# Copying v rows beside turned u rows, so that an expert slot is fetched in one piece of 8 KB instead of two of 4 KB

## The chip, the cores and the metric

The kernel runs on one core of one Trainium2 chip. The metric is device time in microseconds (us): the median of several runs, with one more execution recorded by the hardware profiler. Engines are named as in the profile: PE (TensorE), DVE (VectorE), ACT (ScalarE), POOL (GpSimd), SP (SyncE, which only issues transfers). The profile also counts the core's 16 DMA engines, which move all data between HBM and the on-chip memory.

## The reference

One step of a small backbone with two layers, for 128 context tokens and 256 latent tokens, 384 tokens of 1024 numbers in all, in float32. Each layer runs a mixer (attention, a chunked recurrent scan, a short convolution) and then PEER, a table of 16384 tiny experts per layer. It is PEER's tables that the change touches:

```python
def peer_ffn(h, wq, subkeys, u_tab, v_tab):        # per chunk of 128 tokens
    q = (xt @ wq).reshape(PEER_CHUNK, PEER_HEADS, 2, PEER_HALF)
    sc = jnp.einsum('thpd,hpnd->thpn', q, subkeys)
    ...                                            # top 16 of 256 pairs, per head: expert numbers e, weights g
    act = jax.nn.gelu(jnp.einsum('thkd,td->thk', u_tab[e], xt))
    return jnp.einsum('thk,thkd->td', g * act, v_tab[e])
```

A token has 8 heads with 16 experts each, 128 slots; for every slot a row of u and a row of v (1024 numbers, 4 KB each) are needed. Over 384 tokens and two layers that is 805 MB of gathered rows.

## The kernel before, in words

Tokens lie in 3 tiles of 128, one token per partition. The program runs in stages, each closed by a barrier of all engines: `begin` (once: the input norm and the conditioning products with w_ada, 24 pieces of 1 MB), then for each of the two layers `project` (the input projection, 20 output blocks), `attention`, `rwkv`, `output`, `scoring` (queries, keys, the top 16 of each half), `experts` and `finish`.

**The row turning.** v arrives from the host with one expert per row. u arrives transposed, so each layer turns its u table while the earlier stages run. The table is cut into 128 units, called rows in the code, of 128 experts, 512 KB each. For one unit ACT's queue issues a load into one of 4 buffers (`rows_load`, L261), PE transposes it in 8 pieces of 128x128 into two banks of its own (`rows_pe`, L288), ACT copies the two banks out (`rows_act`, L303) into one of 3 buffers, and ACT's queue issues the store into an HBM tensor `u_rows` (`rows_store`, L274). The load for unit m + 4 is issued behind the copies of unit m; the store of unit m ahead of the copies of unit m + 1; the copies of unit m wait for the store of unit m - 3.

**Where units are turned.** PE and ACT both run their programs in order, and the calls `rows_pe(c, pe, count)` and `rows_act(c, act, count)` stand at fixed places in them. The counts are the constants `IN_BEGIN`, `IN_PROJECT` and so on (L36). Per layer they give: 18 units in `begin` (only in layer 0), 20 in `project` (one behind each output block on PE; on ACT two behind every second block, after that block's weight split L508), 18 in `attention`, 48 in `rwkv`, 8 in `output`, 16 in `scoring`. In layer 0 that is 128. In layer 1 it is 110, and `rows_pe(c, pe, NK)` at the end of `scoring` turns the last 18 there (L1617, L1563). `rows_end` waits until all stores have landed, since `experts` reads the table.

**The experts.** A layer has 384 slots (3 tiles x 128). For each, POOL issues two indirect transfers, one row per token: the u half from `u_rows` and the v half from the input v (L1693), into one of 9 buffers of 128 x 8 KB. For slot n it first waits until PE is done with slot n - 9 (`slot_done`). DVE multiplies the u half with the tokens and sums (L1726), ACT applies the gelu and makes a diagonal matrix of the weights (L1835, L1826), PE multiplies it with the v half and accumulates (L1857). DVE waits for the semaphore `landed` of the u half, PE for `landed_v` of the v half. DVE and ACT take slots in groups of 2, and the weights of a group are made after the next group's sums. Between groups of the first tiles DVE also picks the experts of the next tile (`select`). In layer 0 the weights w_ada of layer 1 come in here too.

Of the kernel before, what the change touches and what calls it, by code (L numbers as in the profile page):

```python
# [10 lines left out]
P = 128  # L11
# [21 lines left out]
SLOTS_OF_TOKEN = PH * TOPK  # L33
GROUP = 2
BUFS = 9
IN_BEGIN, IN_PROJECT, IN_SCORES, IN_VALUES, IN_GRAMS, IN_LEVEL, IN_CHUNKS, IN_SCAN, IN_OUT, IN_Q = 1, 1, 2, 1, 1, 2, 2, 1, 1, 1  # L36

SLOTS = 4
PIECE = 2048
# [66 lines left out]
def make_core(nc, ctx, dram):  # L106
    c = Core()
    c.nc, c.dram = nc, dram
    sb = lambda name, shape, dt=F32: ctx.enter_context(nc.sbuf_tensor(name, shape, dt))
    sem = lambda name: ctx.enter_context(nc.semaphore(name))  # L110
    c.ring = sb("ring", [P, SLOTS, PIECE])
    c.ident = sb("ident", [P, P])
    c.hT = sb("hT", [P, KD, TOK])
    c.mod_cols = sb("mod_cols", [P, 4, KD, 2])
    c.ring_full = [sem(f"ring_full{i}") for i in range(SLOTS)]
    c.att_tables_in, c.rwkv_tables_in = sem("att_tables_in"), sem("rwkv_tables_in")
    c.late_in, c.ident_in = sem("late_in"), sem("ident_in")
    c.rows_came = [sem(f"rows_came{i}") for i in range(ROWS_IN)]
    c.rows_kept = [sem(f"rows_kept{i}") for i in range(ROWS_OUT)]
    c.rows_full, c.rows_free = [[sem(f"rows_{n}{i}") for i in range(2)] for n in ("full", "free")]  # L120
    c.landed = [sem(f"landed{i}") for i in range(BUFS)]
    c.landed_v = [sem(f"landed_v{i}") for i in range(BUFS)]
    c.x_dram = nc.dram_tensor("x_between_blocks", [TILES, P, D], F32, kind="Internal").ap()
    c.gate_dram = nc.dram_tensor("gate_rows", [DEPTH + 1, 2, 2, D], F32, kind="Internal").ap()
    c.u_rows = nc.dram_tensor("u_rows", [DEPTH * NK // 2, P, 2 * D], F32, kind="Internal").ap()
    c.silu, c.ones = sb("cond_silu", [P, KD, 2]), sb("ones", [1, 2])
    return c

# [133 lines left out]
        c.rows_came[m % ROWS_IN], 16)  # L262


def rows_begin(c, act):

    for m in range(c.rows.first, c.rows.first + ROWS_IN):
        rows_load(c, act, m)


def rows_store(c, act, m):

    act.wait_ge(c.rows_free[1], m + 1)
    act.dma_start(c.u_rows[m // 2, :, (m % 2) * D:(m % 2 + 1) * D], c.rows.turned[:, m % ROWS_OUT, :]).then_inc(  # L274
        c.rows_kept[m % ROWS_OUT], 16)


# [15 lines left out]
def rows_act(c, act, count):  # L293

    r = c.rows
    for m in range(r.by_act, min(r.by_act + count, r.end)):
        if m > r.first:
            rows_store(c, act, m - 1)
        if m >= ROWS_OUT:
            act.wait_ge(c.rows_kept[m % ROWS_OUT], 16 * (m // ROWS_OUT))  # L300
        for q in range(2):
            act.wait_ge(c.rows_full[q], m + 1)
            c.nc.scalar.copy(r.turned[:, m % ROWS_OUT, 512 * q:512 * q + 512], r.bank[q][:, :]).then_inc(c.rows_free[q], 1)  # L303
        if m + ROWS_IN < r.end:
            rows_load(c, act, m + ROWS_IN)
    r.by_act = min(r.by_act + count, r.end)


def rows_end(c, act):

    rows_store(c, act, c.rows.end - 1)
    for i in range(ROWS_OUT):
        act.wait_ge(c.rows_kept[i], 16 * len(range(i, c.rows.end, ROWS_OUT)))


def begin(c):

    nc, dram = c.nc, c.dram
    with ExitStack() as ctx:
# [11 lines left out]
        with nc.Block() as block:  # L331
# [15 lines left out]
            def _(act):  # L347
# [11 lines left out]
                    ada_pair_copy(c, s, act, rows, t)  # L359
                for m in range(TILES, N_ADA // PAIR):  # L360
                    ada_pair_copy(c, s, act, rows, m)
                    rows_act(c, act, PAIR * IN_BEGIN)
                for t in range(TILES):
                    act.wait_ge(S["normed"], t + 1)
                    act.dma_start(c.x_dram[t], x[:, t, :]).then_inc(S["stored"], 16)
# [29 lines left out]
            def _(pe):  # L395
# [2 lines left out]
                pe.wait_ge(S["bias_in"], 16)  # L398
                for m in range(N_ADA // PAIR):
                    ada_pair_product(c, s, pe, rows, piece_full, m)  # L400
                    if m >= TILES:
                        rows_pe(c, pe, PAIR * IN_BEGIN)
                ada_transposes(c, s, pe, rows, PAIR)
                pe.wait_ge(S["normed"], TILES)
                for t in range(TILES):
# [37 lines left out]
def project(c, l, pT, att, rw):  # L443
# [3 lines left out]
    with ExitStack() as ctx:  # L447
# [4 lines left out]
        with nc.Block() as block:  # L452
# [8 lines left out]
            def _(act):  # L461
# [5 lines left out]
                for m in range(N_PIN):  # L467
                    b, r = at("proj", 2 * m)
                    act.wait_ge(full[b], r + 1)
                    nc.scalar.copy(pT[:, 2 * m, :], bank[b][:, 0:TOK]).then_inc(free[b], 1)  # L470
                    if m + 2 < N_PIN:
                        split_high(c, s, act, AT_IN, m + 2, ws, at("proj", 2 * m + 1))
                    rows_act(c, act, 2 * IN_PROJECT)

            @block.vector
            def _(dve):
# [1144 lines left out]
def experts(c, l, h_tok, top, idx, acc, late):  # L1621
# [11 lines left out]
    with ExitStack() as ctx:  # L1633
# [28 lines left out]
        shifted = spare(2 * ST).bitcast(U32).rearrange("p (w k) -> p w k", w=2)  # L1662

        BEFORE = l * TILES * ST
        u_rows = c.u_rows[0:(l + 1) * NK // 2].rearrange("a p (two n) -> (a p two) n", two=2)
        v_rows = dram["v"].rearrange("l a p (two n) -> (l a p two) n", two=2)

        def buffer_of(n):
            return uv[(BEFORE + n) % BUFS]
# [12 lines left out]
        with nc.Block() as block:  # L1682

            @block.gpsimd
            def _(pool):
                for n in range(TILES * ST):
# [2 lines left out]
                        pool.wait_ge(S["routed"], 2 * t + 1)  # L1689
                    if n >= BUFS:  # L1690
                        pool.wait_ge(S["slot_done"], n - BUFS + 1)
                    for table, half, came in ((u_rows, 0, c.landed), (v_rows, 1, c.landed_v)):
                        nc.gpsimd.indirect_dma_start(buffer_of(n)[:, half * D:half * D + D], None, table,  # L1693
                                                     bass.IndirectOffsetOnAxis(eid[:, t, k:k + 1], 0)).then_inc(came[landing(n)], 16)

            @block.sync
            def _(sp):
# [150 lines left out]
            def _(pe):  # L1848
                if not last:
                    pe.wait_ge(S["bias_in"], 16)  # L1850
                for j in range(GROUPS):
                    for n in range(j * G, j * G + G):
                        t, k = divmod(n, ST)
                        pe.wait_ge(c.landed_v[landing(n)], landings(n))
                        pe.wait_ge(S["diag_done"], n + 1)
                        for h in range(2):
                            ins = nc.tensor.matmul(acc[2 * t + h][:, :], diag[:, n % DIAGS, :],  # L1857
# [215 lines left out]
```

## Time and profile before

| | us |
|---|---|
| median of 3 runs (3779.28 to 3791.21) | 3790.41 |
| the profiled execution, device time | 3795.43 |
| its span, first to last instruction | 3793.6 |
| busy: PE matmul | 2767.8 (73%) |
| busy: DVE | 1900.8 (50%) |
| busy: POOL | 1615.3 (43%) |
| busy: ACT | 945.0 (25%) |

The profiled execution took 5.0 us more than the median of the three runs. A busy share is an average over stages of very different kinds. The profile has further lines for the DMA engines: their mean busy share over the span in 40 slices, what they moved, and the share of each queue. Queue q0 holds the indirect transfers that POOL issues, q10 the plain ones of ACT, q1 those of SP. PEclk is TensorE's granted clock as a share of full speed.

### The profile page before, as it was taken

What the parts mean: (1) busy time and instruction counts of PE and PEld (TensorE: products, weight loads), DVE (VectorE), ACT (ScalarE), POOL (GpSimd) and SP (SyncE); (2) the same over time, 40 slices, a digit from 0 to 9 for tenths busy, and PEclk for the clock granted to TensorE, in tenths of its full rate; (3) what the DMA queues carried; (4) which work ended last, traced back from release to release, by engine and by line L of the source; (5) the groups of instructions that cost most, each with busy time, mean ns of one, the idle gap of its engine ahead of it and who ended that gap; (6) DMA issues with size and microseconds to landing.
All of it is one profiled execution on the core that took longest, in us unless ns stands there. A gap on an engine that the chain in (4) does not pass through costs nothing. (4 is left out here: it accounts for less than half of the span.)

```text
span 3793.6 us, 36906 instructions
## 1 busy us (share of the span) xinstructions
PE 2767.8 (73%) x12342; PEld 1703.0 (45%) x12342; DVE 1900.8 (50%) x4344; ACT 945.0 (25%) x2400; POOL 1615.3 (43%) x1578
## 2 busy tenths in 40 slices
PE   5686797774777888888758769969366777777775
PEld 3575686761222333333227658859222222222221
DVE  1114655488644444444452355556485444444445
ACT  2334443331111111111123344334211111111111
POOL 0001000006777777777720100000177777777774
PEclk7797798887899999999979779979599999999998
DMA  9756466658999999999975547656799999999996
GB/s 387 304 198 202 139 243 245 230 213 301 351 397 409 411 411 410 410 408 407 409 277 202 185 157 258 233 215 211 275 353 362 400 409 407 409 406 409 408 408 254
DMA packets 323469, 1206.61 MB, mean 318 GB/s; under 512 B 39370, under 2 KB 41930, under 8 KB 311250
## 3 DMA queue, kind: packets, MB, share of 16 engines
q0 software_dynamic: 221184, 805.40, 54.1%
q10 hardware_dynamic: 75328, 274.86, 20.5%
q1 hardware_dynamic: 26772, 123.99, 8.5%
q8 instruction: 103, 1.69, 0.2%
q14 instruction: 82, 0.67, 0.0%
HBM read 1061.47 MB, written 142.64 MB: 317 GB/s over the span
## 5 line engine op out<-in xcount | busy, mean ns | idle before, releaser
L1857 PE MATMUL acc<-exp_uv,exp_diag 128*128 128x512 f32 x3072 | 1462.8, 623 | 618.8 <-ACT exp_diag L1826 618.5
L1726 DVE CUSTOM_DVE_ANT_0 exp_uv<-exp_uv,h_tok 128x1024 f32<-128x1024 f32 x768 | 940.8, 1226 | 1001.9 <-DMA exp_uv<-u_rows,exp_eid 1000.4
L1693 POOL DMA_INDIRECT exp_uv<-u_rows,exp_eid x768 | 784.9, 1022 | 1270.2 <-DVE exp_eid L1801 1006.7
L1857 PEld LDWEIGHTS acc<-exp_uv,exp_diag 128*128 128x128 f32 x3072 | 577.3, 197 | 1492.9 <-issue 1492.9
L1693 POOL DMA_INDIRECT exp_uv<-in_v,exp_eid x768 | 791.8, 1031 | 234.4 <-issue 234.4
L1835 ACT ACTIVATE exp_gel<-exp_dot 128x2 f32<-128x2 f32 x384 | 78.6, 205 | 1732.3 <-DVE exp_dot L1726 1732.3
L303 ACT COPY rows<-rows_bank 128x512 f32<-128x512 f32 x512 | 277.8, 589 | 418.7 <-PE rows_bank L288 312.8
L288 PE MATMUL rows_bank<-ident,rows 128*128 128x128 f32 x2048 | 310.3, 301 | 98.2 <-ACT rows L303 98.2
L288 PEld LDWEIGHTS rows_bank<-ident,rows 128*128 128x128 f32 x2048 | 258.1, 156 | 143.0 <-issue 140.5
L1826 ACT ACTIVATE exp_diag<-ident,exp_w 128x128 f32<-128x128 f32 x768 | 260.9, 388 | 0.1
L552 PE MATMUL project_bank<-project_hs,project_ws 128*128 128x384 f32 x960 | 188.1, 353 | 32.4 <-DVE project_hs L540 32.4
L655 POOL TENSOR_TENSOR att_conv_z<-pT 128x768 f32<-128x768 f32 x2 | 3.6, 1799 | 472.3 <-POOLq L99 472.3
L552 PEld LDWEIGHTS project_bank<-project_hs,project_ws 128*128 128x128 f32 x960 | 176.6, 200 | 33.2 <-DVE project_hs L540 33.2
L552 PE MATMUL score_bank<-score_xs,score_ws 128*128 128x384 f32 x768 | 146.8, 347 | 6.7 <-DVE score_xs L540 6.7
L552 PEld LDWEIGHTS score_bank<-score_xs,score_ws 128*128 128x128 f32 x768 | 137.4, 195 | 7.2 <-DVE score_xs L540 7.2
L1465 PE MATMUL output_bank<-output_ws,output_hs 128*128 128x256 f32 x576 | 81.0, 303 | 39.5 <-DVE output_hs L540 39.2
L483 DVE COPY pT<-project_bank 128x384 f32<-128x384 f32 x20 | 11.2, 558 | 188.8 <-PE project_bank L552 188.8
L1465 PEld LDWEIGHTS output_bank<-output_ws,output_hs 128*128 128x128 f32 x576 | 77.4, 210 | 41.0 <-issue 40.3
L158 PE MATMUL exp_bank<-ring,cond_silu 128*2 128x256 f32 x384 | 86.8, 379 | 0.0
L1277 PE MATMUL rwkv_bank<-rwkv_Dm,rwkv_Ak 128*128 128x128 f32 x480 | 65.6, 300 | 14.1 <-DVE rwkv_Ak L1096 14.1
L1122 DVE TENSOR_TENSOR rwkv_Dm<-rwkv_Dm,rwkv_bank 128x384 f32<-128x384 f32 x64 | 35.2, 549 | 71.3 <-PE rwkv_bank L1289 71.3
L1277 PEld LDWEIGHTS rwkv_bank<-rwkv_Dm,rwkv_Ak 128*128 128x128 f32 x480 | 63.3, 215 | 15.3 <-DVE rwkv_Ak L1096 15.3
(296 smaller groups left out, 2556.0 us busy)
## 6 DMA issues: line engine op xcount, KB each, us to landing
rows<-in_u ACTq DMA_DIRECT2D x256, 512.0 KB, 5.6
u_rows<-rows ACTq DMA_DIRECT2D x256, 512.0 KB, 5.2
ring<-in_w_ada SPq DMA_DIRECT2D x48, 1024.0 KB, 8.0
ring<-in_w_in SPq DMA_DIRECT2D x20, 1024.0 KB, 8.5
ring<-in_wq SPq DMA_DIRECT2D x16, 1024.0 KB, 6.8
exp_uv<-u_rows,exp_eid POOLq DMA_INDIRECT x768, 6.6
exp_uv<-in_v,exp_eid POOLq DMA_INDIRECT x768, 6.6
ring<-in_w_out SPq DMA_DIRECT2D x8, 1024.0 KB, 12.5
```

The lines of the kernel that those rows point to most:

```text
L158: ins = c.nc.tensor.matmul(out, c.silu[:, k, :], w[:, k, :], start=False, stop=(k == KD - 1))
L288: ins = c.nc.tensor.transpose(r.bank[q][:, k * P:(k + 1) * P], r.came_in[:, m % ROWS_IN, f * P:(f + 1) * P], c.ident[:, :])
L303: c.nc.scalar.copy(r.turned[:, m % ROWS_OUT, 512 * q:512 * q + 512], r.bank[q][:, :]).then_inc(c.rows_free[q], 1)
L552: ins = c.nc.tensor.matmul(s.bank[b][:, 0:TOK], w[:, a, n % 2, k, :], hs[:, v, k, :], start=(k == 0 and i == 0), stop=(k == KD - 1 and i = ...
L1122: nc.vector.tensor_tensor(dst[:, g, hh, :, :], dst[:, g, hh, :, :], bank[b][:, 0:TOK].rearrange("p (t n) -> p t n", t=TILES), ALU.add).the ...
L1277: ins = mm(bank[b][:, tile_cols(t)], Ak[:, g, hh, t, :], Dm[:, g, hh, t, :], start=True, stop=True)
L1465: ins = nc.tensor.matmul(bank[b][:, 0:NW], hs[:, v, k, t * P:(t + 1) * P], w[:, a, k, :], start=(k == 0 and i == 0), stop=(k == KD - 1 and ...
L1693: nc.gpsimd.indirect_dma_start(buffer_of(n)[:, half * D:half * D + D], None, table, bass.IndirectOffsetOnAxis(eid[:, t, k:k + 1], 0)).then ...
L1726: V.tensor_tensor_reduce(buffer_of(n)[:, 0:D], buffer_of(n)[:, 0:D], h_tok[:, t, :], 1.0, 0.0, ALU.mult, ALU.add, dot[:, j % 8, n % G:n % ...
L1826: nc.scalar.activation(diag[:, n % DIAGS, :], c.ident[:, :], ACT.Identity, scale=w[:, j % 8, n % G:n % G + 1]).then_inc(S["diag_done"], 1)
L1835: nc.scalar.activation(gel[:, j % 8, :], dot[:, j % 8, :], ACT.Gelu_apprx_tanh).then_inc(S["gelu_done"], 1)
L1857: ins = nc.tensor.matmul(acc[2 * t + h][:, :], diag[:, n % DIAGS, :], buffer_of(n)[:, D + 512 * h:D + 512 * h + 512], start=(k == 0), stop ...
```

## The change

An HBM tensor `uv_rows` takes the place of `u_rows`. Each expert has a row of 8 KB in it, the u row and then the v row. The store of a turned unit writes the u halves. A new transfer per unit (`rows_join`), issued by ACT behind the unit's load, copies the 512 KB of the same experts' v from the input into the v halves, from HBM to HBM; all of them count on one semaphore, `joined`, for which `rows_end` waits. In `experts` POOL issues one indirect transfer per slot, of rows of 8 KB, where it issued two, and DVE and PE wait for the same semaphore.

The places of the units change too. `begin` turns none. `project` turns 40: two behind each output block on PE, and on ACT two right behind each block's copy, one call ahead of the weight split and one behind it. With 18, 48, 8 and 16 in the other stages that is 130 places, so both layers are done with their 128 units two blocks ahead of the end of `scoring`.

```diff
-IN_BEGIN, IN_PROJECT, IN_SCORES, ... = 1, 1, 2, ...
+IN_PROJECT, IN_SCORES, ... = 2, 2, ...
...
-    c.u_rows = nc.dram_tensor("u_rows", [DEPTH * NK // 2, P, 2 * D], F32, kind="Internal").ap()
+    c.uv_rows = nc.dram_tensor("uv_rows", [DEPTH * NK // 2, P, 2, 2, D], F32, kind="Internal").ap()
...
+def rows_join(c, act, m):
+
+    j = m % NK
+    act.dma_start(c.uv_rows[m // 2, :, m % 2, 1, :], c.dram["v"][m // NK, j // 2, :, (j % 2) * D:(j % 2 + 1) * D]).then_inc(c.joined, 16)
...
-    act.dma_start(c.u_rows[m // 2, :, (m % 2) * D:(m % 2 + 1) * D], c.rows.turned[:, m % ROWS_OUT, :]).then_inc(
+    act.dma_start(c.uv_rows[m // 2, :, m % 2, 0, :], c.rows.turned[:, m % ROWS_OUT, :]).then_inc(
...
         if m + ROWS_IN < r.end:
             rows_load(c, act, m + ROWS_IN)
+        rows_join(c, act, m)
...
+    act.wait_ge(c.joined, 16 * c.rows.end)
...
                 for m in range(TILES, N_ADA // PAIR):
                     ada_pair_copy(c, s, act, rows, m)
-                    rows_act(c, act, PAIR * IN_BEGIN)
...
                     ada_pair_product(c, s, pe, rows, piece_full, m)
-                    if m >= TILES:
-                        rows_pe(c, pe, PAIR * IN_BEGIN)
...
                     nc.scalar.copy(pT[:, 2 * m, :], bank[b][:, 0:TOK]).then_inc(free[b], 1)
+                    rows_act(c, act, IN_PROJECT)
                     if m + 2 < N_PIN:
                         split_high(c, s, act, AT_IN, m + 2, ws, at("proj", 2 * m + 1))
-                    rows_act(c, act, 2 * IN_PROJECT)
+                    rows_act(c, act, IN_PROJECT)
...
-                    for table, half, came in ((u_rows, 0, c.landed), (v_rows, 1, c.landed_v)):
-                        nc.gpsimd.indirect_dma_start(buffer_of(n)[:, half * D:half * D + D], None, table,
-                                                     bass.IndirectOffsetOnAxis(eid[:, t, k:k + 1], 0)).then_inc(came[landing(n)], 16)
+                    nc.gpsimd.indirect_dma_start(buffer_of(n)[:, :], None, uv_rows,
+                                                 bass.IndirectOffsetOnAxis(eid[:, t, k:k + 1], 0)).then_inc(c.landed[landing(n)], 16)
...
-                        pe.wait_ge(c.landed_v[landing(n)], landings(n))
+                        pe.wait_ge(c.landed[landing(n)], landings(n))
```

ACT's order in `project`, from the copy of the first output block on. Here `pT` takes the projection, `project_ws` the split weights, and a DMA row is a transfer that ACT's queue issues. Before:

```order
L470 COPY pT<-project_bank 128x384
L508 CAST project_ws<-ring 128x2048
L274 DMA u_rows<-rows 128x1024
L303 COPY rows<-rows_bank 128x512 x2
L261 DMA rows<-in_u 128x1024
L274 DMA u_rows<-rows 128x1024
L303 COPY rows<-rows_bank 128x512 x2
L261 DMA rows<-in_u 128x1024
L470 COPY pT<-project_bank 128x384
```

And in the changed kernel, the same stretch up to the middle of the second half piece:

```order
L475 COPY pT<-project_bank 128x384
L309 COPY rows<-rows_bank 128x512 x2
L261 DMA rows<-in_u 128x1024
L268 DMA uv_rows<-in_v 128x1024
L280 DMA uv_rows<-rows 128x1024
L309 COPY rows<-rows_bank 128x512 x2
L261 DMA rows<-in_u 128x1024
L268 DMA uv_rows<-in_v 128x1024
L514 CAST project_ws<-ring 128x2048
L280 DMA uv_rows<-rows 128x1024
L309 COPY rows<-rows_bank 128x512 x2
```

Between two copies into `pT` ACT had 2 units and 4 transfers; it has 4 units (two stand here ahead of the weight split and two follow behind it) and 12 transfers, the added kind being the copy of v (L268).

PE's order at the end of `begin` and the start of `project` (`begin_bank` takes the conditioning products, `rows_bank` the turned pieces). Before:

```order
L187 MATMUL begin_bank<-begin_rows,ones 2x128 x4
L190 MATMUL begin_bank<-ring,cond_silu 2x128 x32
L288 MATMUL rows_bank<-ident,rows 128x128 x16
L213 MATMUL begin_bank<-ident,begin_rows 128x2 x32
L568 MATMUL begin_bank<-ident,begin_x 128x128 x24
...
L552 MATMUL project_bank<-project_hs,project_ws 128x384 x24
L288 MATMUL rows_bank<-ident,rows 128x128 x8
L552 MATMUL project_bank<-project_hs,project_ws 128x384 x24
```

And in the changed kernel:

```order
L187 MATMUL begin_bank<-begin_rows,ones 2x128 x4
L190 MATMUL begin_bank<-ring,cond_silu 2x128 x32
L213 MATMUL begin_bank<-ident,begin_rows 128x2 x32
L574 MATMUL begin_bank<-ident,begin_x 128x128 x24
...
L558 MATMUL project_bank<-project_hs,project_ws 128x384 x24
L294 MATMUL rows_bank<-ident,rows 128x128 x16
L558 MATMUL project_bank<-project_hs,project_ws 128x384 x24
```

The 16 transposes (2 units) behind each of the last nine conditioning products are gone, and each projection block is followed by 16 instead of 8.

## Rows read from the trace of the kernel before

**Rows 1.** The page's slices of the span: DMA busy tenths, GB/s.

```profile
DMA  9756466658999999999975547656799999999996
GB/s 387 304 198 202 139 243 245 230 213 301 351 397 409 411 411 410 410 408 407 409 277 202 185 157 258 233 215 211 275 353 362 400 409 407 409 406 409 408 408 254
```

**Rows 2.** DMA view, 3000 to 3700 us (experts, layer 1): queue, packets, MB, share of 16 engines.

```profile
q0 software_dynamic: 78381, 285.41, 102.4%
...
exp_uv<-u_rows,exp_eid POOLq DMA_INDIRECT x273, 6.6
exp_uv<-in_v,exp_eid POOLq DMA_INDIRECT x273, 6.6
```

**Rows 3.** Costliest groups, same stretch: busy, mean ns of one, idle before and releaser.

```profile
L1857 PE MATMUL acc<-exp_uv,exp_diag 128*128 128x512 f32 x1089 | 502.9, 605 | 198.8 <-ACT exp_diag L1826 198.8
L1726 DVE CUSTOM_DVE_ANT_0 exp_uv<-exp_uv,h_tok 128x1024 f32<-128x1024 f32 x272 | 333.3, 1226 | 354.1 <-DMA exp_uv<-u_rows,exp_eid 354.1
L1693 POOL DMA_INDIRECT exp_uv<-u_rows,exp_eid x273 | 279.1, 1022 | 83.1 <-issue 83.1
L1693 POOL DMA_INDIRECT exp_uv<-in_v,exp_eid x273 | 256.7, 940 | 83.3 <-issue 83.3
```

**Rows 4.** DMA view, 60 to 120 us (begin): queue, packets, MB, share.

```profile
DMA packets 5193, 25.22 MB, mean 420 GB/s; under 512 B 579, under 2 KB 579, under 8 KB 3661
...
q10 hardware_dynamic: 3469, 12.63, 51.7%
q1 hardware_dynamic: 1718, 12.50, 49.6%
```

**Rows 5.** Stretches: length, busy of PE, PEld, DVE, ACT, POOL (instructions), PEclk, DMA share, GB/s.

```profile
2667.00:2703.00 36.00, 24.68 (x112) 20.06 (x110) 0.30 (x3) 15.05 (x29) 0.00 (x0) 0.59 0.98 398
154.00:282.00 128.00, 106.93 (x622) 103.88 (x620) 23.92 (x18) 40.56 (x57) 0.00 (x0) 0.93 0.60 206
1990.00:2114.00 124.00, 103.03 (x619) 100.15 (x617) 23.92 (x18) 40.11 (x57) 0.00 (x0) 0.96 0.59 206
2800.00:2900.00 100.00, 68.05 (x136) 26.68 (x136) 74.34 (x180) 16.32 (x54) 79.59 (x68) 0.93 0.96 352
```

**Rows 6.** Timeline, last product of begin: start, length, engine, line, idle before and releaser.

```profile
114.72 3.59 PE L190 MATMUL begin_bank<-ring,cond_silu 128*2 128x128 f32 x64
118.40 0.59 ACT L303 COPY rows<-rows_bank 128x512 f32<-128x512 f32 x1 [5.75 <-DMA u_rows<-rows]
...
122.67 2.10 PE L213 MATMUL begin_bank<-ident,begin_rows 2*128 2x2 f32 x32
```

**Rows 7.** Timeline, end of scoring in layer 1.

```profile
2667.02 0.28 DVE L1587 FIND_INDEX8 idx<-top,score_sc 128x8 uint32<-128x128 f32 x1
...
2702.48 0.33 ACTq L274 DMA_DIRECT2D u_rows<-rows  x1
2706.72 0.33 SPq L1698 DMA_DIRECT2D exp_iota<-in_iota  x1
```

**Rows 8.** Timeline, a pair of units in project.

```profile
176.44 1.07 ACT L303 COPY rows<-rows_bank 128x512 f32<-128x512 f32 x2
...
177.16 1.94 PE L288 MATMUL rows_bank<-ident,rows 128*128 128x128 f32 x8 [2.62 <-ACT rows L303]
177.53 0.33 ACTq L274 DMA_DIRECT2D u_rows<-rows  x1
```

**Rows 9.** Line L303 alone (two copies per unit) by stretch: ACT busy (count), PEclk, DMA share, GB/s.

```profile
350.00:377.00 27.00, 8.66 (x16) 0.98 0.84 267
484.00:536.00 52.00, 17.20 (x32) 1.00 0.86 300
590.00:624.00 34.00, 10.75 (x20) 1.00 0.80 281
657.00:714.00 57.00, 8.61 (x16) 0.89 0.69 278
722.00:834.00 112.00, 17.22 (x32) 0.93 0.63 221
```

More of the change, by code:

```diff
@@ L35 @@
 BUFS = 9
-IN_BEGIN, IN_PROJECT, IN_SCORES, IN_VALUES, IN_GRAMS, IN_LEVEL, IN_CHUNKS, IN_SCAN, IN_OUT, IN_Q = 1, 1, 2, 1, 1, 2, 2, 1, 1, 1
+IN_PROJECT, IN_SCORES, IN_VALUES, IN_GRAMS, IN_LEVEL, IN_CHUNKS, IN_SCAN, IN_OUT, IN_Q = 2, 2, 1, 1, 2, 2, 1, 1, 1
 SLOTS = 4
@@ L121, in make_core @@
     c.landed = [sem(f"landed{i}") for i in range(BUFS)]
-    c.landed_v = [sem(f"landed_v{i}") for i in range(BUFS)]
+    c.joined = sem("joined")
     c.x_dram = nc.dram_tensor("x_between_blocks", [TILES, P, D], F32, kind="Internal").ap()
     c.gate_dram = nc.dram_tensor("gate_rows", [DEPTH + 1, 2, 2, D], F32, kind="Internal").ap()
-    c.u_rows = nc.dram_tensor("u_rows", [DEPTH * NK // 2, P, 2 * D], F32, kind="Internal").ap()
+    c.uv_rows = nc.dram_tensor("uv_rows", [DEPTH * NK // 2, P, 2, 2, D], F32, kind="Internal").ap()
     c.silu, c.ones = sb("cond_silu", [P, KD, 2]), sb("ones", [1, 2])
@@ L1664, in experts @@
         BEFORE = l * TILES * ST
-        u_rows = c.u_rows[0:(l + 1) * NK // 2].rearrange("a p (two n) -> (a p two) n", two=2)
-        v_rows = dram["v"].rearrange("l a p (two n) -> (l a p two) n", two=2)
+        uv_rows = c.uv_rows[0:(l + 1) * NK // 2].rearrange("a p two w n -> (a p two) (w n)")
         def buffer_of(n):
```

## The prediction

> **What bounds the kernel now.** I began with the slices of the span [rows 1]. They show two long plateaus, slices 12 to 20 and 32 to 39, at 397 to 411 GB/s with the DMA engines at nine tenths or more: the two `experts` stages. Between them the engines are half idle (139 to 304 GB/s), except in the first slice and at the end of the second `scoring`. So the reader should see two kinds of stage, and ask of each edit in which kind it lies.
>
> For the plateau I took a calm stretch without expert picking. In 700 us POOL issues 273 u fetches and 273 v fetches, so a slot takes 2.564 us; the indirect queue is busy for 102.4% of the stretch and moves 285.41 MB, that is 285.41 / (1.024 x 700 us) = 398 GB/s of full share [rows 2]. The groups say the rest [rows 3]: PE is busy for 503 of 700 us and DVE for 333, DVE's idle time ends on the fetch, PE's on ACT's diagonals, which follow DVE. POOL has no gap either: 279.1 + 256.7 busy and 83.1 + 83.3 of issue make 702 us. The v issues take 940 ns and the u issues 1022, so POOL alone could go at 2 x (0.940 + 0.305) = 2.49 us a slot. Transfers and their issue both stand close to the slot's 2.56 us, and a gain there needs both.
>
> For the other kind I took the price of one 512 KB transfer with the DMA engines full. In `begin`, ACT's queue moves 12.63 MB in 51.7% of 60 us, 407 GB/s of full share; SP's queue, whose pieces are 8 KB, moves 12.50 MB in 49.6%, 420 GB/s [rows 4]. At the end of `scoring` in layer 1 ACT's transfers alone make 398 GB/s at a share of 0.98, 406 again [rows 5]. So a load or a store of a unit costs 0.524 MB / 407 GB/s = 1.29 us, and a turned unit 2.58 us of the DMA engines. In `project` the share is only 0.60 and 0.59 [rows 5]: there the units are hidden today.
>
> **The change, part by part. The first stage.** 18 units leave `begin`, where the DMA engines are full: 18 x 2.58 = 46 us. PE's last product starts at 114.7 us, and the transposes behind it, at 122.7, follow a unit that waited 5.75 us for a store [rows 6]. What is late next is w_ada itself: a pair of pieces, 2.1 MB at 420 GB/s, takes 5.0 us against 3.59 us of product, so the DMA engines still set the pace and nearly all of the 46 come out. I take -45.
>
> **The end of scoring.** In layer 1 DVE is done at 2667.3 us; the last store is issued at 2702.5 and `experts` starts at 2706.7 [rows 7]. These 39 us go, less some 2 for the barrier: -37. Two units fewer inside each `scoring` save PE a little, -2 per layer.
>
> **The fetch.** The bytes stay. If an 8 KB row gains as SP's 8 KB pieces do over ACT's 4 KB pieces, 420 / 407 = 1.032, the slot falls from 2.564 to 2.485 us, -0.08 x 768 = -61 us. If it went at 420 GB/s outright it would be 1.049 MB / (420 x 1.024) = 2.44 us, -96; if the row is moved as two pieces as before, nothing. Issue no longer holds it: one issue in place of two is about 1.3 us per slot. While DVE picks experts the rate is only 352 GB/s at a share of 0.96 [rows 5], and there the gain is smaller. I take -55, with 0 and -96 as ends. DVE now waits for the v half too; behind it in its program stand the next sums and weights, and PE waits for those, but the DMA engines move the same bytes in a slot, so this costs one half fetch at the start of a layer, about 1.3 us, which I leave out.
>
> **The copy of v.** No row shows an HBM to HBM transfer. It cannot be cheaper than one pass, 1.29 us, the price of the same 128 pieces of 4 KB as a load or as a store. If its reading and its writing come one after the other in whatever is full, it costs a load and a store, 2.58 us. What is nearest? In `begin` loads and stores are mixed, at the end of `scoring` they are half and half, in `experts` there are loads alone, and all come to 398 to 420 GB/s of HBM reading plus writing [rows 2, 4, 5]. A store's write does not ride free beside a load's read. An engine that is busy per piece would look the same, so these rows do not decide it; I take 2.58, since by count of HBM bytes the copy is nearest to a unit's load and store. The Trainium skill's page DMA: Bandwidth & Descriptors, section Latency and other measured facts, has 207 to 214 GB/s per direction for copies between two HBM tensors. By it the copy would be 0.524 MB / 214 = 2.45 us, an estimate, and the sum below 20 us less; no run here shows it yet.
>
> The copies are issued on ACT's queue, ahead of later loads and stores. PE meets a unit in its program order and waits for its load; behind it stand the projection's blocks. So a full queue stops the projection itself.
>
> **Project.** The share of 0.60 over 128 us is 77 us of transfers: 20 units x 2.58 = 52, and 25 for w_in and tables [rows 5]. Afterwards it is 40 x (2.58 + 2.58) + 25 = 231 us. Some lies outside: four loads are issued ahead, and the last stores and copies land later; I count three units, 15 us. 216 in place of 128 is +88 us per layer (+40 with the cheap copy: 40 x 3.87 + 25 - 12 = 168). PE is not the bound: a unit with its wait on ACT takes it at most 1.94 us [rows 8], so 20 more are 39 us, 167 in all. ACT's issues take 0.33 us each and its copies 0.59 [rows 6, 8]; 40 units x (2 x 0.59 + 3 x 0.33) is 87 us, well inside.
>
> **The other stages.** Their units stay, but each brings a copy. The dense runs [rows 9], where two copies on ACT are one unit: 16 units from 484 to 536 us need 0.86 x 52 + 16 x 2.58 = 86 us, 34 too much, of which three units (15) can wait in buffers: +19. From 590 to 624: 27 + 10 x 2.58 = 53, +4 by the same rule. From 350 to 377: 23 + 8 x 2.58 = 43, +1. `output`: 39 + 21 = 60 in 57, +3. In `scoring` 0.63 x 112 + 14 x 2.58 - 2 x 2.58 = 102 stays under 112 and is hidden; that slack also covers the new wait for `joined`, since the last unit comes two blocks before the end. Together +27 per layer, or +2 with the cheap copy.
>
> **The sum.** 2 x (88 + 27) = +230; -45 - 37 - 4 - 55 = -141; net +89. 3795.4 + 89 = 3884 for a profiled execution; the median lay 5.0 below its profile, so 3880 us, 2.4% slower.
>
> **The rivals.** *The copy costs one pass.* Then a layer loses 40 + 2, two lose 84, and the gains of 141 win: -57, 3733 us. For it speaks that each load and store now fills the engines alike, whichever end is HBM, as if the pieces were the cost. Against it, the byte count above. The line between: the loss per layer goes from 42 to 115 while the copy goes from 1.29 to 2.58, and it equals half of 141 at about 1.8 us. Below that the change is faster.
>
> *The wide fetch gains nothing*, because each row is still moved as two pieces, or because nine buffers, of which a slot now holds one until the whole row is there, hold POOL back. POOL never waits for PE in the calm stretch [rows 3], which speaks against the second. With the dear copy: 3880 + 55 = 3935.
>
> *The turned units stay hidden.* This is the hope that the half-idle stages have room: per layer `project` to `scoring` has it on average. It needs the copies to be spread; in `project` alone they ask for more than the stage has, so I see it only as part of the cheap copy: a price of about 1.8 us, 3790 us, no change.
>
> **How the numbers follow.** Dear copy with the gain 0.51 (3880; its own range 3850 to 3920), dear copy without it 0.09 (3935), near the line 0.07 (3790), cheap copy 0.33 (3733, or 3710 to 3760 by the fetch's ends). A measurement of this kernel tells about 0.3%, 11 us, from no change. Faster 0.33, same 0.07, slower 0.60. The range 3720 to 3940 leaves out the tails of the outer cases, below 2 in 10.
>
> **What would show it.** Right: in the two `project` stages a DMA share near 1, PE waiting for units on the load of u, some 215 us in place of 128 in each; ACT's queue with a third of transfers more and at 2 to 2.6 us each; `begin` ending near 78 in place of 123 us; `experts` following `scoring` without the 39 us; a slot at 2.45 to 2.5 us. Wrong: a copy at 1.3 us with `project` near 170 us; a slot that stays at 2.56; `begin` still ending past 100 us, if PE or ACT take over there.

## The result and the profile after

The changed kernel takes 3742.54 us, the median of 4 runs (3735.49 to 3744.95), beside 3790.06 us for the kernel before on the same chip: a ratio of 0.9878 with a 95% interval of 0.9855 to 0.9901, 1.2% faster where 2.4% slower was forecast. It came out 9.5 us above the first rival, the copy that costs one pass (3733). The profiled execution took 3744.95 us, its span 3743.1; before it was 3795.4, so 50.5 us went.

The slices of the changed kernel's span, DMA busy tenths and GB/s, answer to [rows 1]:

```profile
DMA  8997599686999999999969876986689999999996
GB/s 346 368 404 265 214 364 332 266 304 260 420 420 419 417 416 420 418 417 419 420 271 404 340 272 230 345 323 264 229 329 420 420 415 420 420 417 420 416 415 249
```

The plateaus of `experts` went from some 408 to some 419 GB/s, and `project` (slices 3, 22 and most of 23, counted from one) became full. Stage by stage, from the first to the last instruction with the turned units left aside, read from the two timelines (us). `project` counts from its first to its last copy into `pT`, `output` from its first product to its last step on ACT ahead of the norm (`output_rstd`):

| stage | before, layers 0 / 1 | after | change |
|---|---|---|---|
| start to the first copy of `pT` in `project` | 155.0 | 120.3 | -34.7 |
| project | 126.6 / 123.4 | 155.3 / 154.9 | +28.7 / +31.5 |
| project's end to attention | 2.6 / 2.4 | 7.0 / 7.3 | +4.4 / +4.9 |
| attention | 90.8 / 91.6 | 101.2 / 106.5 | +10.4 / +14.9 |
| rwkv | 270.6 / 270.5 | 276.1 / 279.2 | +5.5 / +8.7 |
| output | 57.3 / 56.8 | 63.0 / 63.7 | +5.7 / +6.9 |
| scoring | 111.8 / 111.9 | 110.6 / 110.8 | -1.2 / -1.1 |
| scoring's end to experts, layer 1 | 39.4 | 1.7 | -37.7 |
| experts | 1106.1 / 1057.3 | 1057.5 / 1008.1 | -48.6 / -49.2 |

**Project.** The DMA view of the changed kernel, 130 to 250 us (layer 0): queue, packets, MB, share of 16 engines; then issues by kind with the median time to landing.

```profile
q10 hardware_dynamic: 12351, 44.96, 93.7%
q1 hardware_dynamic: 576, 4.19, 8.4%
...
uv_rows<-rows ACTq DMA_DIRECT2D x29, 512.0 KB, 10.0
rows<-in_u ACTq DMA_DIRECT2D x29, 512.0 KB, 8.9
uv_rows<-in_v ACTq DMA_DIRECT2D x29, 512.0 KB, 10.1
```

29 stores, 29 loads and 29 copies share the queue, and 44.96 MB / (0.937 x 120 us) is 400 GB/s: 0.524 MB / 400 = 1.31 us of the engines for each transfer, close to the 1.29 of [rows 4], with a third of them copies. The times to landing (8.9 to 10.1 us) are some seven times this price: about as many transfers are under way at once, an estimate. The stretches of the changed kernel (columns of [rows 5]) show the half-idle stages filled, and the waits of 120 to 276 us show what ends ACT's waiting there:

```profile
120.00:276.00 156.00, 128.41 (x770) 122.85 (x768) 23.92 (x18) 60.37 (x95) 0.00 (x0) 0.92 1.02 405
1960.00:2115.00 155.00, 124.49 (x768) 119.19 (x767) 23.64 (x18) 60.04 (x94) 0.00 (x0) 0.94 1.02 407
283.00:384.00 101.00, 68.81 (x403) 56.69 (x404) 38.80 (x94) 42.11 (x111) 15.65 (x17) 0.70 0.77 274
388.00:664.00 276.00, 219.08 (x1734) 194.71 (x1734) 157.03 (x318) 105.33 (x225) 2.87 (x2) 0.89 0.81 295
743.00:854.00 111.00, 96.94 (x616) 95.99 (x616) 80.94 (x395) 49.39 (x77) 0.00 (x0) 0.93 0.75 270
```

```profile
ACT rows L309 <- DMA uv_rows<-rows: 56.2, 29, 4.6
...
PE rows_bank L294 <- ACT rows L309: 27.4, 21, 2.7
```

ACT waits for the store of a unit three before, which lies in the queue behind copies. PE's own waits there end on ACT's copies out of its banks, and none is put down to a load. The transfers alone fill the stage: from the first to the last copy into `pT` the q10 queue moves 57.30 MB, 109 of the 120 transfers, at 1.31 us each, and w_in takes 13 us more, 156 in all.

**The fetch.** The DMA view of 2950 to 3650 us (a calm stretch, as [rows 2]), POOL's group there (as [rows 3]), and the stretch with expert picking that [rows 5] has at 352 GB/s:

```profile
q0 software_dynamic: 40106, 292.09, 101.0%
...
exp_uv<-uv_rows,exp_eid POOLq DMA_INDIRECT x279, 11.6
```

```profile
L1697 POOL DMA_INDIRECT exp_uv<-uv_rows,exp_eid x279 | 294.1, 1054 | 407.6 <-PE acc L1861 404.1 <-issue 3.5
```

```profile
2800.00:2900.00 100.00, 75.15 (x158) 29.83 (x159) 78.06 (x193) 18.74 (x63) 44.64 (x40) 0.97 1.01 420
```

A slot takes 700 / 279 = 2.509 us, 0.055 less. POOL, which had no gap, now waits 404 of 700 us for PE to free a buffer: issue has stopped being a limit. In the picking stretch it had been the limit: 68 issues of 79.59 us together and 0.3 us of issue time after each fill the 100 us of [rows 5]. Now 40 issues of 44.64 us suffice, and the stretch moves 420 GB/s in place of 352, 40 slots in place of 34. The next tiles' experts are picked while some 50 slots at the start of each layer are worked off; the first 96 slots of a layer gained 32 us, the other 288 some 18.

**The first stage.** PE's last product of `begin` and what follows it, as [rows 6], and two stretches ahead of it; then the waits of 20 to 92 us on SP:

```profile
88.37 3.27 PE L190 MATMUL begin_bank<-ring,cond_silu 128*2 128x128 f32 x64
93.03 2.42 PE L213 MATMUL begin_bank<-ident,begin_rows 2*128 2x2 f32 x32 [1.39 <-ACT begin_rows L200]
```

```profile
40.00:60.00 20.00, 9.18 (x236) 5.94 (x228) 0.00 (x0) 4.11 (x16) 0.00 (x0) 0.83 0.82 321
60.00:80.00 20.00, 10.51 (x216) 6.37 (x216) 0.00 (x0) 2.64 (x11) 0.00 (x0) 0.68 0.79 318
```

```profile
SPq L350 <- PE begin_bank L190: 54.8, 9, 9.0
```

The transposes start at 93.0 in place of 122.7 us. The engines are not full any more: SP may not issue a pair of pieces before the product of the pair that held its place in the four-slot ring, and spends 54.8 us on that.

### The profile page after: what moved, and what is told of

Its sections match the earlier page's. It is cut to its first block and busy times, and to the rows that moved or that the text cites. A ratio compares the mean times of both kernels' runs of the same rounds, so it can differ in the third digit from the quotient of the medians.

```text
span 3743.1 us, 36396 instructions
## 1 busy us (share of the span) xinstructions
PE 2738.1 (73%) x12342; PEld 1698.9 (45%) x12342; DVE 1901.3 (51%) x4344; ACT 940.4 (25%) x2400; POOL 884.8 (24%) x810
## 5 line engine op out<-in xcount | busy, mean ns | idle before, releaser
L1861 PE MATMUL acc<-exp_uv,exp_diag 128*128 128x512 f32 x3072 | 1431.9, 612 | 559.3 <-ACT exp_diag L1830 559.3
L1697 POOL DMA_INDIRECT exp_uv<-uv_rows,exp_eid x768 | 846.1, 1102 | 2115.8 <-PE acc L1861 1102.2
L1861 PEld LDWEIGHTS acc<-exp_uv,exp_diag 128*128 128x128 f32 x3072 | 566.3, 193 | 1413.4 <-issue 1413.1
L294 PE MATMUL rows_bank<-ident,rows 128*128 128x128 f32 x2048 | 295.9, 292 | 102.1 <-ACT rows L309 101.8
L294 PEld LDWEIGHTS rows_bank<-ident,rows 128*128 128x128 f32 x2048 | 246.3, 150 | 142.8 <-issue 139.9
L521 DVE TENSOR_TENSOR project_ws<-ring,project_ws 128x2048 fp32r<-128x2048 f32 x20 | 45.8, 2292 | 39.4 <-ACT project_ws L514 39.4
```

Of the source, the lines that this page charges most:

```text
L294: ins = c.nc.tensor.transpose(r.bank[q][:, k * P:(k + 1) * P], r.came_in[:, m % ROWS_IN, f * P:(f + 1) * P], c.ident[:, :])
L521: c.nc.vector.tensor_tensor(ws[:, b, 1, :], c.ring[:, slot(first + m), :], ws[:, b, 0, :].bitcast(F32), ALU.subtract).then_inc(s.named["w_ ...
L1697: nc.gpsimd.indirect_dma_start(buffer_of(n)[:, :], None, uv_rows, bass.IndirectOffsetOnAxis(eid[:, t, k:k + 1], 0)).then_inc(c.landed[land ...
```

## The experiments

**Theory**: a copy of v costs the DMA engines about what a load costs, so the loss is small and the one fetch pays for it. **Rivals**: the copy is dear, and something else gave the time; `project` is long because of 20 more units on PE and ACT, not because of the copies; the fetch is worth only its 2.2% in a calm slot.

**move** is the kernel before with the placement alone:

```diff
-IN_BEGIN, IN_PROJECT, ... = 1, 1, ...
+IN_PROJECT, ... = 2, ...
...
+                    rows_act(c, act, IN_PROJECT)
                     if m + 2 < N_PIN:
...
-                    rows_act(c, act, 2 * IN_PROJECT)
+                    rows_act(c, act, IN_PROJECT)
```

> Only the placement of the turning is changed: none in begin, two half pieces a block in project, no unit left behind scoring. u is stored in its old table, v is not copied, a slot is fetched in two 4 KB halves as before. The first stage should end about 35 us earlier and the 38 us behind the second scoring should go, -75 together with scoring itself. Theory that the copies are what lengthens project: project needs 62 - 21 = 41 MB at 400 GB/s, 103 us, is again bound by PE and ACT and takes 126 to 140 us a layer; attention, rwkv and output stay at 91, 271 and 57; total 3715 to 3745. Rival, that the twenty additional units a project lengthen it by their turns on PE and ACT whatever the copies do: project at 155 us as in the changed kernel, total about 3775.

3738.48 us, ratio 0.9861 (0.9828 to 0.9894). `project` takes 135.2 us a layer, attention 94.8, rwkv 270.6, output 57.4. Its stretch:

```profile
119.00:254.00 135.00, 116.83 (x766) 112.01 (x765) 23.88 (x18) 59.90 (x95) 0.00 (x0) 1.00 0.93 328
```

So the units alone lengthen `project` by some 10 us and the copies by 20, and the placement alone has the whole net gain. Of attention's loss 3 to 4 us a layer come with the placement too. PE's granted clock is 1.00 here and 0.92 in the changed kernel's `project`, where PE is busy for 128 us in place of 117; but there the transfers alone add up to the stage's length.

**two_fetches** is the changed kernel with u and the copied v in two tables and two 4 KB fetches a slot:

```diff
-    c.uv_rows = nc.dram_tensor("uv_rows", [DEPTH * NK // 2, P, 2, 2, D], F32, kind="Internal").ap()
+    c.u_rows = nc.dram_tensor("u_rows", [DEPTH * NK // 2, P, 2 * D], F32, kind="Internal").ap()
+    c.v_rows = nc.dram_tensor("v_rows", [DEPTH * NK // 2, P, 2 * D], F32, kind="Internal").ap()
...
-                    nc.gpsimd.indirect_dma_start(buffer_of(n)[:, :], None, uv_rows,
+                    for table, half, came in ((u_rows, 0, c.landed), (v_rows, 1, c.landed_v)):
+                        nc.gpsimd.indirect_dma_start(buffer_of(n)[:, half * D:half * D + D], None, table,
```

> The changed kernel with u and v rows in two tables and a slot fetched in two 4 KB halves; the copies of v and the placement stay. Theory that the 98 us that both experts stages lost came from the one 8 KB fetch: experts back at 1106 and 1057 us, a calm slot at 2.56 us, the stretches with expert picking back at 352 and 375 GB/s; total 3742 + 98 = 3840. Rival, that the fetch is worth the 2.2 per cent of the calm slot alone (0.055 us x 768 = 42 us) and the rest came with the placement: 3785.

3835.72 us, 1.0135 (1.0095 to 1.0174). `experts` is back at 1107.8 and 1049.4 us, and its picking stretch (the same place in layer 1) at 361 GB/s with POOL full:

```profile
2842.00:2942.00 100.00, 71.14 (x139) 27.80 (x138) 75.37 (x180) 17.08 (x57) 78.84 (x70) 0.91 0.97 361
```

The theory holds: the one fetch is worth 3835.7 - 3742.5 = 93 us. And with two fetches on both sides, the copies cost 3835.7 - 3738.5 = 97 us in all. The two halves of the table cancel.

**old_places** completes the square: copies and one fetch, with the units placed as before.

```diff
+                    rows_act(c, act, PAIR * IN_BEGIN)
...
+                    if m >= TILES:
+                        rows_pe(c, pe, PAIR * IN_BEGIN)
```

> The other half of the change alone: v copied beside u and one 8 KB fetch a slot, with the turning placed as in the kernel before (18 units in begin, one half piece fewer in project, a tail behind scoring). The placement alone gave 3738, both together 3743, the kernel before 3790. If the two halves add, this one is worth about +4: 3794. If the copies in begin and in the tail behind the second scoring, where the DMA engines are full, cost more than those that leave project: 18 x 1.3 and 10 x 1.3 us, less up to 2 x 20: 3790 to 3800. If the fetch's 98 us were had for less there: below 3770.

3786.97 us, 0.9981 (0.9959 to 1.0003): no change that can be told. `begin` ends 22 us later than before (first `pT` copy at 177.2) and the wait behind the second scoring grows from 39 to 65 us, where the copies meet full engines (a DMA share of 1.02 in `begin`, 0.98 behind `scoring`), while `project` with its 20 units stays at 125.0. So placement is worth 52 us without the table and 44 with it.

**copies_alone** issues layer 0's 128 copies in a stage of their own, ahead of `begin`.

```diff
+            for m in range(NK):
+                rows_join(c, act, m)
+            act.wait_ge(c.joined, 16 * NK)
...
-        rows_join(c, act, m)
+        if m >= NK:
+            rows_join(c, act, m)
```

> A stage ahead of the first one issues layer 0's 128 copies of v one behind the other, with nothing else on the DMA engines; layer 0's other stages then carry no copies, layer 1 is as in the changed kernel. One pass a copy: 128 x 1.31 = 168 us for the stage, near 400 GB/s; and with layer 0 losing its 50 us (project 155 to about 130, attention 101 to 91, rwkv 276 to 271, output 63 to 57), total 3742 + 168 - 50 = 3860. A load and a store a copy: 128 x 2.58 = 330 us, total about 4020. The Trainium skill, page DMA: Bandwidth & Descriptors, section Latency and other measured facts, has 207 to 214 GB/s for HBM to HBM; by it the stage would be 67.1 MB / 214 = 314 us, an estimate.

3904.97 us; the stages that follow start 215 us later, and layer 0's `project` takes 135.1 us, as in `move`. The DMA view of 20 to 200 us:

```profile
q10 hardware_dynamic: 16009, 58.30, 100.8%
```

58.30 / (1.008 x 180) = 321 GB/s, 1.63 us a copy: between the theories, and dearer than the 1.31 of `project`. The Trainium skill's page DMA: Bandwidth & Descriptors, section Latency and other measured facts, has 214 GB/s per direction as the full rate of copies between HBM tensors, measured on pieces of 16 KB at a padded row pitch of 4 MB. These copies, of 4 KB pieces that lie closer, went well above it, and for them the measurement decides.

**prices, prices_paced, prices_long** ask why. Each adds a stage with nothing else on the engines and issues transfers in a chosen order, the first with the queue full, the second with at most four under way, the third with 128 rounds in `project`'s order. The first lines are of `prices`, the others of `prices_long`.

```diff
+            for m in range(3 * each, 4 * each):
+                load(m, range(4))
+                store(m, range(4, 7))
+                rows_join(c, act, m)
...
+            for m in range(NK):
+                store(m, range(4, 7))
+                load(m, range(4))
+                rows_join(c, act, m)
```

> A stage ahead of the first one, with nothing else on the DMA engines, issues 512 KB transfers on ACT's queue in five stretches, each waited out: 32 copies of v alone; 32 times a copy and a load; a copy and a store; a load, a store and a copy; a load and a store. Layer 0's later stages carry no copies. 128 copies alone took 1.62 us each and a transfer of the changed kernel's project 1.31. Theory that a copy is dear among copies only and costs one pass beside other transfers: 52, 83, 83, 125 and 83 us. Rival, that a copy always takes 1.62 and the loads and stores of project were cheaper: 52, 93, 93, 135 and 83.

> The five stretches of 512 KB transfers again (copies; copy and load; copy and store; load, store and copy; load and store), with at most four transfers under way where the first run of them let ACT's queue fill, about nine. There they took 56.8, 96.4, 91.2, 134.2 and 82.6 us, so a copy 1.55 to 1.78 us, while project of the changed kernel came out at 1.31 a transfer. Theory that the copies grow dear in a deep queue: 32 x 1.31 = 42 us and some 2 of latency for the copies alone, then 84, 84, 126 and 83. Rival, that a copy has its price of about 1.6 whatever is queued, and project has another reason: 55, 95, 91, 134, 83; with the latency of four in flight showing, more.

> The order of project without PE and ACT's work: a stage ahead of the first issues store, load and copy 128 times over, then 64 copies in order, then 64 copies in the order 0, 64, 1, 65, on ACT's queue, each stretch waited out. In project a transfer came out at 1.31 us; in the first run of prices 32 rounds of load, store and copy took 1.40 a transfer, and copies alone 1.62 to 1.78, with four under way 1.81. If that order and the address of the unit don't matter: 537, 104 to 114 and 104 to 114 us. If the order of project is what makes its copies cheap: 503 us for the first stretch. If the copy's price hangs on the addresses that are under way together: the two stretches of copies differ by more than 5 us.

The insides of the stretches. `prices`: copies; copy and load; copy and store; load, store and copy; load and store:

```profile
4.00:56.00 52.00, 0.00 (x0) 0.00 (x0) 0.00 (x0) 0.00 (x0) 0.00 (x0) 1.00 0.98 311
65.00:153.00 88.00, 0.00 (x0) 0.00 (x0) 0.00 (x0) 0.00 (x0) 0.00 (x0) 1.00 1.00 363
165.00:246.00 81.00, 0.00 (x0) 0.00 (x0) 0.00 (x0) 0.00 (x0) 0.00 (x0) 1.00 1.03 380
258.00:382.00 124.00, 0.00 (x0) 0.00 (x0) 0.00 (x0) 0.00 (x0) 0.00 (x0) 1.00 1.02 388
392.00:466.00 74.00, 0.00 (x0) 0.00 (x0) 0.00 (x0) 0.00 (x0) 0.00 (x0) 1.00 1.02 417
```

`prices_paced`: copies alone; load, store and copy; load and store:

```profile
6.00:57.00 51.00, 0.00 (x0) 0.00 (x0) 0.00 (x0) 0.00 (x0) 0.00 (x0) 1.00 0.98 295
...
276.00:424.00 148.00, 0.00 (x0) 0.00 (x0) 0.00 (x0) 0.00 (x0) 0.00 (x0) 1.00 0.95 326
...
430.00:516.00 86.00, 0.00 (x0) 0.00 (x0) 0.00 (x0) 0.00 (x0) 0.00 (x0) 1.00 1.00 378
```

`prices_long`, store, load and copy (its start and the rest), 64 copies in order, 64 in the order 0, 64, 1, 65:

```profile
10.00:50.00 40.00, 0.00 (x0) 0.00 (x0) 0.00 (x0) 0.00 (x0) 0.00 (x0) 1.00 1.02 339
50.00:500.00 450.00, 0.00 (x0) 0.00 (x0) 0.00 (x0) 0.00 (x0) 0.00 (x0) 1.00 1.02 411
520.00:615.00 95.00, 0.00 (x0) 0.00 (x0) 0.00 (x0) 0.00 (x0) 0.00 (x0) 1.00 1.01 327
630.00:725.00 95.00, 0.00 (x0) 0.00 (x0) 0.00 (x0) 0.00 (x0) 0.00 (x0) 1.00 1.02 302
```

Rate by share gives a transfer's price: load and store 0.524 MB / (417 / 1.02) = 1.28 us, the three together 1.38 in `prices`, 1.30 in `prices_long`. With 1.28 for a load or a store, the copy costs 1.58 there and 1.34 here; beside loads 1.60, beside stores 1.56, alone 1.62 to 1.77. From first to last piece the stretches of `prices` took 57, 97, 91, 134 and 83 us, as its rival had it: in those orders a copy was dear beside other transfers too.

The depth theory fell: with four under way copies alone cost 1.74 and the three together 1.53 each, more, not less. Loads and stores paid as well, 1.39 in place of 1.28, which leaves 1.8 for the copy among the three.

The first stretch of `prices_long` took 503 us from its first piece to its last, as the theory of the rotation had it. But order and length were changed at once, and its first 40 us run at 339 GB/s too, as the first 20 us of the three together in `prices` run at 363 and the rest at 380 to 396. So what is shown is that a long steady rotation comes to one pass a copy, and copies in a row do not. The two stretches of copies took 108 and 118 us from first to last piece, 10 apart where the expectation asked for 5: in this one run (302 and 327 GB/s inside) the order of the addresses mattered too, and what makes copies in a row dear stays open. In the rotation 95% of the 4 KB pieces take 159 or 160 ns, so most of the copies' pieces too. Amid copies alone, over all runs, 59 to 74% of them still do, but the slow ones bring the mean to 202 to 218.

**late_copies, pool_copies, spread_copies, some_in_scoring** try to place the copies better: fewer in `project`, more where engines idle. In the first, ACT issues 20 of them later, in scoring; in the second POOL issues all; in the third and fourth `project` keeps 20 and 28 of its 40 and POOL issues those of scoring (in the third also 4 in `begin` and 6 in `finish`).

```diff
-        rows_join(c, act, m)
+    rows_joins(c, act, count if joins is None else joins)     # late_copies
...
+    if m >= AHEAD:                                            # pool_copies
+        pool.wait_ge(c.joined[m % AHEAD], 16 * (m // AHEAD))
+    pool.dma_start(c.uv_rows[m // 2, :, m % 2, 1, :], ...
...
+        if m % 10 < each and c.by_join < r.end - POOL_SCORING:   # some_in_scoring
+            rows_join(c, act, c.joined)
```

> The changed kernel with 20 of the 40 copies of each project issued in scoring instead, where the DMA share is 0.75 of 111 us. If project is held by its transfers alone, it loses 20 x 1.31 = 26 us a layer and scoring hides them in its 28 idle us: total 3742 - 52 = 3690. If PE and ACT take over in project: at most half of that, 3715. If scoring pays for the copies that it takes: 3742, no change.

> The changed kernel with the copies of v on POOL's queue, two under way at a time, none of them in project: 12 at the end of begin, 16 in finish ahead of layer 1, 24 in attention, 60 in rwkv, 8 in output, the others in scoring. If the copies cost only where they stand ahead of loads and stores in ACT's queue or meet full DMA engines, the stages return to those of the kernel with the placement alone (135, 95, 271, 57 and 111 us) and the experts keep 1058 and 1008: 3743 - 86 = about 3657. If they take their bytes from the stages wherever they are issued: 3743. With half of the loss left: 3700.

> The changed kernel with the copies placed where the runs found room: in project one for every second unit, behind it in ACT's queue as before; attention, rwkv and output unchanged; in scoring 28 to 30 on POOL's queue, two under way, and none on ACT's; 4 at the end of begin and 6 in finish on POOL's queue. With 20 copies fewer project took 142 us in place of 155, and scoring held 24 copies on POOL's queue at an unchanged 110.7 us: 3743 - 2 x 13 = 3717. If the copies that leave project lengthen scoring or delay the ends of begin and finish: 3743 or more.

> The changed kernel with 12 of the 40 copies of each project left to scoring, which issues its 26 on POOL's queue, two under way, and none on ACT's; nothing in begin and finish. Scoring held 24 to 28 such copies at 110.5 to 110.7 us. Theory that project is held by its transfers: 12 x 1.31 = 16 us less a layer, at most, and half of that since the rotation of store, load and copy is broken (late_copies moved 378 GB/s there in place of 405): 3743 - 16 = 3727, faster than both kernels and than the placement alone, 3738. Rival, that what project gives comes back in the stages behind it, as in the two kernels that moved 20 copies (project 25 us shorter, the whole 19 and 31 us longer): 3750.

3773.31 us (0.9956, 0.9940 to 0.9971), 3811.50 (1.0053, 1.0029 to 1.0076), 3761.14 (0.9913, 0.9883 to 0.9944), 3759.45 (0.9905, 0.9881 to 0.9930): all slower than the changed kernel. Every one of their runs lies above its highest, 3745, though the last two intervals overlap with its own. `late_copies` and `pool_copies` were slower than all that was expected of them, and of the other two the theory that moving copies pays fell. All four also change which unit's v is copied beside a unit, and `late_copies` puts two units' copies one behind the other elsewhere too. `project` of layer 0 in `late_copies`, then in `some_in_scoring`:

```profile
120.00:262.00 142.00, 119.79 (x763) 114.69 (x762) 23.36 (x17) 60.08 (x94) 0.00 (x0) 0.98 1.02 378
```

```profile
123.00:281.00 158.00, 123.92 (x761) 118.77 (x760) 23.51 (x18) 59.71 (x94) 0.00 (x0) 0.95 1.00 366
```

The engines stay full while the rate falls from 405 to 378 and 366: with 20 copies fewer `project` gains 13 us and not 26, and with 12 fewer, the rotation broken in three units of ten, nothing (158.7 and 152.1 us in place of 155). That would fit an even rotation that is itself worth something; the other addresses would do as well, and no run tells the two apart. What did come was given back. In `late_copies` scoring took 131.8 and 126.3 us, since ACT stood in its own issues and waited for stores, and DVE's scores waited behind it (the view of layer 0's `scoring`):

```profile
DVE top L1599 <- ACT score_sc L1571: 35.2, 7, 9.8
ACT score_sc L1571 <- issue: 31.2, 8, 7.7
ACT rows L317 <- DMA uv_rows<-rows: 22.9, 6, 7.2
```

In `pool_copies` `project` fell to 135.2 and scoring held 24 copies at 110.7, but POOL's paced copies outlasted `begin`, attention and `finish` (22, 23 and 36 us at their ends), and rwkv, with 60 copies in place of 48, took 289.6 and 281.3. In `spread_copies` layer 0's last copies came 17 us behind scoring; rwkv of layer 1 took 289.8. With the same 48 copies rwkv took 284.6 and 285.5 in `late_copies`, 284.0 and 280.5 in `some_in_scoring`, in place of 276.1 and 279.2; why isn't known.

**few_in_begin** puts seven units back into `begin`:

```diff
+IN_PAIR = {4: 1, 6: 1, 8: 1, 10: 1, 11: 3}
...
+                    rows_act(c, act, IN_PAIR.get(m, 0))
```

> The changed kernel with 7 units of layer 0 turned in begin: one behind each second pair of w_ada, where the DMA share is 0.8, and three behind the last pair, where it falls to 0.54. If they lie in DMA time that begin leaves unused, project of layer 0 has 33 units and falls from 155 to about 155 - 7 x 3 x 1.31 = 128, held at 135 by PE and ACT, and begin stays: 3743 - 20 = 3723. If begin pays 1.94 us a unit as it paid in the kernel before (35 us for 18 units): 3743 - 20 + 14 = 3737. If both project and begin keep their loads' price: 3743.

3756.95 us, 0.9908 (0.9892 to 0.9925), 14 more than the changed kernel. All three expectations had the place wrong: `project` takes two units a half piece whatever went before, so it stayed at 156.4 us and the seven left scoring, which fell to 104.8. `begin` paid 22.8 us, 3.3 a unit.

## Why the prediction was wrong

**The copy of v is the step that failed.** It was priced at 2.58 us, "since by count of HBM bytes the copy is nearest to a unit's load and store". In `project` a transfer took 1.31, a third of them copies (1.37 for the copy if the others kept 1.28, an estimate); alone a copy took 1.63, and nowhere 2.58. The dearest, with four under way, came to 3 x 1.53 - 2 x 1.39 = 1.8, where the prediction turned. The count of bytes was the wrong measure: a full `project` moves some 528 GB/s of reading plus writing and not 405, since a copy's bytes are counted once there and both read and written. The engine's time per piece is what the rows of loads and of stores had in common, the other reading that the prediction named and did not take: 159 ns is the median of a 4 KB piece in `begin` of the kernel before, in the long rotation and among copies alone.

**Project** came out at +29 and +31, not +88, and below the +40 of the cheap copy: 155 us for 168. The 25 us that the sum put down to w_in and tables were 13. The engines are full, as said; but the wait that was named, PE's for loads, did not come: ACT waits for stores, and PE for ACT.

**The other stages** lost 22 and 30 us a layer, near the +27 of the dear copy and far from the +2 of the cheap one. The engines have room there (0.77, 0.81); what the copies do is stand ahead of a unit's store and load in ACT's queue. `pool_copies` took them out of that queue, and `output`, with the same 8, was longer (73.7 and 72.5 us, for 63.0 and 63.7); attention was shorter (97.5 and 96.5) but left copies over behind it. So the queue's order alone isn't the cause; which part is order and which the copies' slower pieces stays open. Another 9 us came at the two ends of `project`, 7 in place of 2.5 us each, which the sum had not counted.

**The fetch** was the right mechanism with the wrong size: -98, not -55. The calm slot fell by 0.055 us, 42 us over 768 slots, below the 0.08 used. The other 56 lie almost all where "the gain is smaller" was written: in picking stretches POOL's issue was the limit, which [rows 5] showed in POOL's 79.59 us with 68 issues, and one issue in place of two removed it.

**Begin** gave 34.7 of 45. The limit "if PE or ACT take over there" came, as a third thing: the ring, by SP's waits; no run has a longer one. **The end of scoring** gave 37.7 (37) and the units inside it 2.3 (4). The four gains sum to -172 in place of -141, the losses to +122 in place of +230: -50.

**Of the rivals**, the cheap copy is what happened, with the fetch larger and the other stages dearer than it had them. Its gains were 31 us too small and its losses 38 too small, so that 3733 lies so near is in part luck. "The wide fetch gains nothing" is refuted by `two_fetches`. "The turned units stay hidden" is refuted by `project`.

## What to carry to other kernels

Before pricing an HBM to HBM copy, time it in the order in which it will be issued: here it cost one pass in an even rotation with loads and stores, and a quarter to a third more in a row. Look in every stretch, not on average, for which of issue and transfer is the limit; merging two fetches paid most where issue was. And split a change into its halves: the placement alone (3738.5 us) is as fast as the whole (3742.5), and the table's copies, 97 us, eat the 93 that its fetch gives.

## What was not expected of the hardware

The rate of full DMA engines depends on the pattern: 417 GB/s for loads and stores in turn, 411 with copies in an even rotation, 366 to 378 with the rotation broken and other addresses, 302 to 327 for copies in a row, and 378 for loads and stores with at most four under way, at a share of about 1.0 each time. A busy share of 1 doesn't say that the bytes are moving as fast as they can. And ACT itself stops in its issues when enough transfers are under way: in `copies_alone`, where it waits for nothing else, the first 14 issues took 0.6 to 0.7 us each and the 18th 4.9, with some 13 copies under way. In `late_copies` 31 us of scoring went there.
